# Probabilities times v in the third mixer: one head at a time, or both heads of a pair in turns

## The reference, cut to what matters

```python
q, k = rms_norm_2(q, q_norm_g), rms_norm_2(k, k_norm_g)     # per head, 64 features
s = q @ k.T * HEAD_DIM ** -0.5                              # -inf where key position > query position
p = softmax(s)
y_att = (p @ v) * silu(ga)                                  # the change: how p @ v is issued
y = concatenate([y_lru, y_att]) @ w_out
x = x + gate * y
```

## Time and profile before

| what | value |
|---|---|
| median of 3 runs | 2309.34 us (2305.47 to 2311.35) |
| time of the profiled execution | 2308.53 us |
| its span in the trace | 2306.7 us |
| PE busy | 2252.1 us (98% of the span) |
| DVE busy | 1270.6 us (55%) |
| ACT busy | 906.2 us (39%) |
| mean granted TensorE clock | 0.992 |
| third mixer's attention steps | about 2133 to 2271 us of the span |

### The profile page before, as it was taken

One profiled execution on the slowest core, in us unless ns is written; L12 is line 12 of the kernel. 1 busy time (PEld: TensorE's weight loads), 2 busy tenths in 40 slices (PEclk: granted clock), 3 DMA queues, 4 the chain that ended last, 5 costly groups with the idle time before them and its releaser, 6 DMA issues.

```text
span 2306.7 us, 24697 instructions
## 1 busy us (share of the span) xinstructions
PE 2252.1 (98%) x9842; PEld 1799.0 (78%) x9842; DVE 1270.6 (55%) x1970; ACT 906.2 (39%) x1402; POOL 154.0 (7%) x127
## 2 busy tenths in 40 slices
PE   7999999899899999999999999999899999999999
PEld 6888887776677888888888887777688888877777
DVE  6443445777754434455433445877566535655763
ACT  4222333545433222233322324777533223237662
POOL 2000002000040000020000012000030000020000
PEclk9999999999999999999999999999999999999999
DMA  5323224021023323233223224222135433232211
GB/s 187 101 82 110 96 69 148 19 92 55 26 80 128 117 91 110 82 101 109 82 83 128 78 80 133 71 71 89 37 112 163 139 117 128 89 126 73 74 55 37
DMA packets 201746, 217.39 MB, mean 94 GB/s; under 512 B 4968, under 2 KB 194536, under 8 KB 201632
## 3 DMA queue, kind: packets, MB, share of 16 engines
q1 hardware_dynamic: 194960, 193.48, 25.9%
q0 software_dynamic: 6528, 22.26, 2.9%
q10 hardware_dynamic: 144, 0.08, 0.0%
HBM read 213.66 MB, written 6.32 MB: 95 GB/s over the span
## 4 chain that ended last, share of the span: by engine, by line
PE 89%; DVE 6%; ACT 3%; issue 2%; DMA 0%; SPq 0%; DVEq 0%; ACTq 0%
PE ps L1574 88%; PE ps L1578 1%; DVE sb_wlo L1043 1%; ACT sb_whi L607 1%; DVE sb_gla_ek L1280 0%; DVE sb_gla_at L1295 0%; DMA sb_raw<-ffn_w_gu 0%; ACT sb_xh L607 0%; DVE sb_xl L1048 0%; DVE sb_gla_eq L1283 0%; DVE sb_gla_xb L1275 0%; DVE sb_gla_d L1262 0%; ACT sb_hyb_th L607 0%; DVE sb_gla_on L1206 0%; ACT sb_gla_z L607 0%
## 5 line engine op out<-in xcount | busy, mean ns | idle before, releaser
L1574 PE MATMUL ps<-sb_xh,sb_whi 128*128 128x512 f32 x2120 | 849.2, 401 | 22.7 <-DVE sb_xl L1048 9.8
L1574 PE MATMUL ps<-sb_xh,sb_wlo 128*128 128x512 f32 x2120 | 831.1, 392 | 0.0
L1574 PE MATMUL ps<-sb_xl,sb_whi 128*128 128x512 f32 x2120 | 830.7, 392 | 0.0
L1043 DVE TENSOR_TENSOR sb_wlo<-sb_raw,sb_whi 128x1024 fp32r<-128x1024 f32 (+2 forms) x401 | 475.2, 1189 | 524.6 <-ACT sb_whi L607 523.4
L607 ACT ACTIVATE sb_whi<-sb_raw 128x1024 fp32r<-128x1024 f32 (+2 forms) x401 | 387.2, 968 | 604.9 <-PE ps L1574 596.4
L1574 PEld LDWEIGHTS ps<-sb_xh,sb_whi 128*128 128x128 f32 x2120 | 402.0, 190 | 117.8 <-issue 17.1
L1574 PEld LDWEIGHTS ps<-sb_xl,sb_whi 128*128 128x128 f32 x2120 | 401.8, 190 | 86.9 <-issue 6.0
L1574 PEld LDWEIGHTS ps<-sb_xh,sb_wlo 128*128 128x128 f32 x2120 | 401.1, 189 | 85.9
L1574 PE MATMUL ps<-sb_ffn_ah,sb_whi 128*128 128x512 f32 x704 | 277.6, 394 | 0.0
L1574 PE MATMUL ps<-sb_ffn_ah,sb_wlo 128*128 128x512 f32 x704 | 276.0, 392 | 0.0
L1574 PE MATMUL ps<-sb_ffn_al,sb_whi 128*128 128x512 f32 x704 | 273.3, 388 | 0.0
(11 more groups left out here) (249 smaller groups left out, 1775.6 us busy)
## 6 DMA issues: line engine op xcount, KB each, us to landing
sb_raw<-ffn_w_gu SPq DMA_DIRECT2D x86, 1024.0 KB, 5.2
sb_raw<-ffn_w_down SPq DMA_DIRECT2D x32, 1024.0 KB, 4.9
sb_raw<-gla_w_in SPq DMA_DIRECT2D x12, 1024.0 KB, 5.3
sb_raw<-diff_w_in SPq DMA_DIRECT2D x12, 1024.0 KB, 5.1
sb_ada_raw<-w_ada POOLq DMA_DIRECT2D x12, 1024.0 KB, 6.4
sb_raw<-w_in SPq DMA_DIRECT2D x10, 1024.0 KB, 5.3
sb_raw<-ffn_w_down SPq DMA_DIRECT2D x16, 512.0 KB, 3.5
sb_raw<-ffn_w_down SPq DMA_DIRECT2D x16, 256.0 KB, 2.7
```

What stands on the lines that cost most here:

```text
L1043: e.tensor_tensor(lo, raw[panel % NRAW][:, 0:nk, off:off + 128], hi.bitcast(F32), ALU.subtract).then_inc(sem["w_lo"], 1)
L1574: return e.matmul(out, lhsT, rhs, start=start, stop=stop, skip_group_check=skip)
```

## The change

`hybrid_block(n)` is new and tells all engines which pair, head, query block and number of keys block n is. The order of the blocks in a pair becomes head 0 queries 0 and 1, head 1 queries 0 and 1, head 0 queries 2 and 3, head 1 queries 2 and 3. N becomes 128, 256, 128, 256, 384, 512, 384, 512. `HPT` then holds 256 queries of each of the two heads (columns 256k on), and `pv(o)` makes these 256 queries of both heads: for each chunk of keys one matmul for head 0 and one for head 1, so that consecutive instructions write partitions 0 to 63 and 64 to 127 in turns.

```diff
+def hybrid_block(n):
+
+    qt = n // 4 % 2 * 2 + n % 2
+    return n // 8, n // 2 % 2, qt, 128 * (qt + 1)
...
                     elif s[0] == "turn":
                         n = s[1]
-                        qt = n % 4
+                        _, k, qt, N = hybrid_block(n)
+                        at = 256 * k + qt % 2 * 128
...
-                        act(HPT[:, 0:qt + 1, qt * 128:qt * 128 + 128],
-                            psum[HYB_TURN][:, 0:128 * (qt + 1)].rearrange("p (c q) -> p c q", q=128),
+                        act(HPT[:, 0:qt + 1, at:at + 128],
+                            psum[HYB_TURN][:, 0:N].rearrange("p (c q) -> p c q", q=128),
                             ACT.Copy).then_inc(sem["h_pt"], 1)
...
                     elif s[0] == "pv":
                         o = s[1]
-                        i, k = o // 2, o % 2
+                        i, g = o // 2, o % 2
                         w.wait_ge(sem["h_vrow"], i + 1)
                         w.wait_ge(sem["h_pt"], 4 * o + 4)
-                        if i and k == 0:
+                        if i and g == 0:
                             w.wait_ge(sem["h_ya"], i)
-                        for c in range(4):
-                            ins = mm(psum[HYB_PV][64 * k:64 * k + 64, c * 128:S], HV[i % 2][:, c, 64 * k:64 * k + 64],
-                                     HPT[:, c, c * 128:S], c == 0, c == 3, True)
+
+                        last = 2 * g + 1
+                        for c in range(last + 1):
+                            q0 = 128 if c == last else 0
+                            for k in range(2):
+                                ins = mm(psum[HYB_PV][64 * k:64 * k + 64, 256 * g + q0:256 * g + 256],
+                                         HV[i % 2][:, c, 64 * k:64 * k + 64], HPT[:, c, 256 * k + q0:256 * k + 256],
+                                         c == 0, c == last, True)
                         ins.then_inc(sem["h_pv"], 1)
```

## The result

The changed kernel took 2298.82 us (median of 6 runs, 2295.38 to 2303.28), the kernel before beside it 2309.88 us (2305.47 to 2312.61). The ratio is 0.9955, with a 95% interval of 0.9943 to 0.9968: faster by 0.45%, 10.4 us. The forecast was 2302.3 us in a range from 2299.5 to 2310.0.

A forecast was written before the change was run, and what follows sets the result against it. PE was taken to bound the kernel, busy 98% of the span. The profiled 2308.53 us less 6.5 for overlap and 0.5 for block order gave 2301.5, as a median 2302.3 us, range 2299.5 to 2310.0.

The forecast's parts named there:

- What bounds the kernel: Whole span: PE is busy 98% at full clock, so PE work saved counts one for one where PE never waits.
- Serially: pv without overlap: streaming stays 4.30 us per pair, 1.29 and 3.01; 32 more records cost about 0.1 us.
- If the halves overlap: pv matmuls: in-order issue, B1 starting with A2, saves 6.9 us, 4.5 with every load exposed; 6.5 taken, chance 0.65.
- the best case: pv overlap with no extra record at the start: half of the serial time, 8.6 us saved.
- the one on distinct column groups: Skill's rule for pv: small outputs in distinct column groups run 2.38 times faster for three; gain 6 to 8 us.
- the one on row groups: Skill's rule for pv: loads overlap matmuls only in different row groups, so every load is exposed and nothing gained.
- The order of the blocks: Start of attention: smaller blocks 2 and 3 bring PE's wait before the third transposes earlier, 0.5 us gained.
- DVE covers it: Larger blocks 4 and 5: their extra work fits DVE's idle time before block 7, leaving 2.2 of 4.49 us.
- The tail: End of the kernel: the weight's wait for a slot hangs on PE and moves with it, otherwise unchanged.
- one after the other: Rival for pv: the halves do not overlap for fp32, only 0.5 us remains, 2308.8 us; chance 0.20.
- each turn costs: Rival for pv: each change of half drains the array, 0.14 us or more, 2314.4 to 2318.0 us; chance 0.09.
- given back: Rival: halves overlap, but fuller DVE and ACT make PE wait, returning 1.0 us a pair, 2306.3 us; chance 0.06.

The follow-up runs named there:

- short turns: The changed kernel with each pv matmul of 256 columns cut into two of 128, still alternating between heads: 2302.23 us, executed once.
- the repeat: The changed kernel measured once more, unaltered, against the kernel before: 2299.68 us (6 runs), ratio 0.9966.
- Head by head: The changed kernel with each pv issuing all chunks of head 0, then all of head 1: 2303.46 us, ratio 0.9983.
- unequal widths: The changed kernel with head 1's pv matmuls always 128 columns wide, head 0's kept at 256: 2299.55 us, executed once.
- quarters: The changed kernel with each head's 64 features split into two pv matmuls of 32: 2301.46 us, executed once.
- three and three: The changed kernel with a second pv issuing three chunks of head 0, three of head 1, then each one's last: 2304.28 us, executed once.
- two and two: The changed kernel with a second pv issuing two chunks of head 0, two of head 1, and again: 2296.42 us, executed once.

## Why the prediction was wrong, step by step

That the halves overlap was right, the size of the gain was not: the term for the overlap stood at 6.5 us and measured 8.52, the term for the order of the blocks stood at 0.5 and measured nothing. The second miss hid part of the first, so 7.0 us were forecast and 8.44 were there.

*What bounds the kernel* held. PE's time off is the kernel's time off: 8.52 us of `pv` became 8.44 us from the first scores to the end, and in the third and fourth stretch PE is still busy all of the time.

*Serially* held: with one half used, 1.45 and 3.17 us against 1.29 and 3.01 of streaming plus 0.14 of edge. Cutting 8 matmuls into 12 costs 0.08 us in all (the eight `pv` sum to 18.46 instead of 18.39), where 0.1 was forecast.

*If the halves overlap* was the step that failed, in size. "Instructions go in order ... B1 may start with A2" is false: B1 overtakes A2. I charged one record at each start for it (8.6 to 6.9) and then took 0.4 off for loads in the open, so the term stood at 6.5 us and measured 8.52. The bound that I had called the best case, half of the serial time, is what happened. The load is in the open once per half and `pv`, in both halves at the same time, not 48 times. My 0.05 per matmul came from the only load that has nothing running beside it, though the earlier trace rows showed all others starting under a matmul. Of the two rules that I had weighed there (the Trainium skill, TensorE: Matmul & The Clock Gate, Part 3), the trace agrees with the one on distinct column groups: a pair's two `pv` took 4.60 us before and 2.47 after. By the one on row groups, loads of matmuls that all use 128 rows would not be hidden; short turns hid them behind records of 0.109 us, and the measurement decides.

*The order of the blocks* was worth nothing, not 0.5 us. The waits that I followed did shrink: before the transposes of block 1 and 2, PE now waits 0.45 and 0.82 us instead of 0.66 and 0.95, though I had put the second under 0.6. But a new one of 0.20 us stands before those of block 3:

```profile
2145.54 0.41 PE L1585 MATMUL ps<-sb_cst,sb_hyb_p 128*128 128x128 f32 x2 [0.20 <-ACT sb_hyb_pt L613]
```

PE's holes up to the first `pv` went from 27.42 - 25.43 = 1.99 to 26.97 - 25.11 = 1.86 us. The first `pv` starts 0.45 us sooner, but only 0.13 of that is holes, and the rest is transposes that moved behind it (blocks 0 to 3 have 6 pieces now, not 10), and they are paid for in the next stretch. I had counted a chain's shift as a gain without the work that PE itself put off. With one half alone the same order gave 179.62 us, no gain at all.

*DVE covers it* held. Its idle time before block 7's maximum was forecast at 2.2 us and is 2.61:

```profile
2151.68 0.69 DVE L1507 CUSTOM_DVE_ANT_0 sb_hyb_p<-ps,sb_hyb_causal 128x512 f32<-128x512 f32 x1 [2.61 <-PE ps L1581]
```

*The tail* is unchanged: the chain has ACT's weight, DVE's rest and 22.24 us of PE as in the earlier trace rows. Of the rivals, "one after the other" would have been 179.6 us from the first scores on, "each turn costs" has no cost per turn: the second half starts 0.007 us after the first and stays 0.005 to 0.007 behind through all 16 records; "given back" did not happen: beyond that 0.20 the wait before the second `pv` grew from 0.47 to 0.63 us, but PE's idle time from the first scores on fell from 7.01 to 6.84.

*The range* failed by the sum of this and of something that was not in it. Best case for overlap, 8.6 us, gave 2300.7 us without the 0.5 of the order; the true effect, 8.44 on a median of 2309.34, is 2300.9. The first comparison measured 10.4 us, the repeat 7.9 (0.9966), and the trace says 8.44: the median of 2298.82 was some 2 us on the lucky side. Against the 2308.36 us of the 21 later runs of the kernel before, instead of the three runs that I had, 8.44 would have led to 2299.9, and the repeat's 2299.68 lies inside the range: on which side of 2299.5 the time fell was chance, the size of the term was not. The scatter goes with the clock's dips. Sorted by the mean granted clock of the execution, 0.990 to 0.994 in steps of 0.001, the kernel before took 2310.8, 2309.7, 2308.3, 2306.2 and 2304.0 us (means of the 21 runs), the changed one in the repeat 2302.1, 2301.3, 2298.1, 2298.1 and 2295.7 (6 runs): at each clock it is 8.1 to 10.2 us faster. No run was made to hold the clock. The low end at 2299.5 left about 1 us for it, while the kernel before alone spread over 7 us in its runs.

## What to carry to other kernels

Where a product has 64 or fewer output partitions, put another such product into the other half of the array and let their instructions stand close: here in turns, or with at most four records (two fp32 matmuls) of one half in a row, which cost 0.05 us where it came twice. Only fp32 was tried, on an engine that was busy all of the time. Bounds of an unseen overlap should not be shaded towards the middle by a cost that the rows show only at its edge. A range for a change of 0.3% has to hold the scatter of the comparison itself, and the trace from the first changed instruction on is the better scale: it repeated to 0.01 us where single times spread over 8.

## What the runs showed of the hardware

- A matmul that uses other columns overtakes waiting ones, if at most three records before it wait. Head by head, unequal widths, quarters, three and three, and two and two fit this; where it was used to forecast, it hit 2.15 and 173.0 us and missed 1.67 by 0.05. Each fp32 product is two records here, so a limit of one whole waiting product fits all of it as well, and whether loads are counted was not tried.
- Weight loads of the two halves run beside each other: two loads in the open at a start hold up their halves by 0.05 us together, not one after the other, and 28 records of 128 columns start two by two every 0.109 us, with loads of 0.137.
- Four streams of fp32 in four quarters run side by side at the pace that one half has alone: 32 records in 1.65 us.
- Going over to another half costs nothing per turn, only the 0.007 us by which the second half starts later; going into and out of the 64-column form costs 0.14 a time as before.
